# A hybrid encoder block on one core: the hidden layer of the feed-forward part formed in seven products from the third group on, with VectorE squaring its positive part in one pass

## The chip, the core and the metric

One core of a Trainium2 chip runs one program. The metric is the device time of an execution in microseconds (us). Engines: PE is TensorE (matmul), DVE VectorE, ACT ScalarE, POOL GpSimd, SP SyncE, which here only issues DMAs. They share no clock of work: each runs its own queue in order, and they meet through semaphores.

## What is computed

```python
h2 = modulate(rmsnorm(h_res, pre_ffn_g[l]), sh2, sc2)
f = jnp.square(jax.nn.relu(h2 @ w_ff1[l])) @ w_ff2[l]
h_res = h_res + gt2[:, None, :] * rmsnorm(f, post_ffn_g[l])
```

This is the channel sub-layer, the last third of a layer. The input h2 has 1024 tokens and 1024 features, w_ff1 is 1024 x 4096, w_ff2 4096 x 1024. Before it comes the mixing sub-layer (retention, stick-breaking attention, gates, an output projection), which the change leaves alone.

## The kernel before

Every fp32 product is made of three fp32r matmuls: each operand is kept as a high part (rounded by a copy) and a low part (the rest), and PE adds high x high, high x low and low x high into a PSUM bank. For weights ACT makes the high part (`w_high`, L1243) and POOL the low part (`low`, L489), 128 x 1024 elements, one **unit**, at a time; for the squares of the hidden layer ACT makes the high part (`f_high`, L1270) and DVE the low part (`f_low`, L1759).

The feed-forward part walks over 8 **groups** of 512 hidden features. A group has two halves.

- **Hidden** (`ff_hidden` on PE, L908, by way of `tile`, L543): 8 tiles, 4 blocks of 128 features by 2 halves of the tokens, each 8 chunks x 3 = 24 matmuls of 128 x 128 weights by 512 tokens, into the four banks `pg`. The operand is `r_hi`, `r_lo` (h2, transposed, 64 KB a partition). ACT takes each bank with Relu into `hid` and squares it there (`hidden`, L1253).
- **Second products** (`product`, L923): `hid` is cut in 2 x 2 blocks a11 to a22 and the 512 x 1024 part of w_ff2 likewise in b11 to b22, and seven products stand for eight (Strassen's scheme in Winograd's form). In PE's order they are P1, P4, P6, P5, P7, P3, P2, each 4 banks x 2 chunks x 3 = 24 matmuls. P1, P6, P7, P2 go to the banks `px`, P4, P5, P3 to `pg`; P6 and P7 add to what lies there, so each waits for the eviction of what came before. POOL makes the four sums of weight blocks, DVE the four sums of hidden blocks (a21, s2, a11, s2 again, L1781 to L1798) and the 32 evictions that add banks into `y` (`evict`, L1764). The last group makes its 16 tiles plainly (`ff_last`, L949).

Group 0 is written out, groups 1 to 6 are one loop on each engine, group 7 is `ff_last`. SP's queue (L404 to L427) loads the units of the next group as slots come free: two slots `raw` for w_ff1, four slots `w2` for w_ff2. The order on every queue is written out by hand. What makes ACT wait is gemm_done (PE's count of finished tiles) for a free slot, ff_sq for the squares, ff_s and ff_t for the sums.

One line says how a product waits; `free` gives the eviction that must be done:

```python
pe.wait_ge(ff_wlo, FF_UNITS * g + 4 + i + 1)
pe.wait_ge(ff_lo, FF_PRODS * g + i + 1)
```

After the last tile DVE and ACT normalise the rows of y and SP stores them (`finish`, `finish_last`).

## Time and profile before

| | |
|---|---|
| three executions | 1746.11, 1748.28, 1748.68 us, median 1748.28 |
| the profiled execution's own time | 1748.37 us |
| its span (first to last instruction) | 1746.6 us |
| busy in the span | PE 1709.1, DVE 905.0, ACT 561.3, POOL 604.2 us |
| mean granted clock of PE | 0.996 |
| feed-forward part | from about 1071 us to the end |

The profile is of one execution. Its page gives busy times, the chain of work that ended last (followed back from the last instruction), and groups of instructions by line with their mean duration and what ended the idle time before them. Beside it the trace can be asked for tables by stretches of time, for the instructions of one engine in order of time, and for those of one line. A matmul's duration of about 0.4 us there is its way through the pipeline; starts lie closer than that.

### The profile page before, as it was taken

Reading aid. Unit: us, or ns where it says so; the run is one execution under the profiler, and the core shown is the slowest. Engines: PE = TensorE matmul, PEld = TensorE weight load, DVE = VectorE, ACT = ScalarE, POOL = GpSimd, SP = SyncE. Lnnn points to the kernel's source line nnn. Section 1 sums busy time; section 2 is a strip of 40 time slices with the busy share of each in tenths; the row PEclk is TensorE's granted clock in tenths of the full one; section 3 lists DMA queues with packets and bytes.
Section 4 is the critical chain, followed back from the end, with each engine's and each line's share of the span. In section 5 each row is a group of like instructions: output and inputs, shape, how many; then the busy total and the mean of one; then the engine's idle time right before and its main releaser. Section 6 shows DMA issues by size and latency. Waiting matters only on the chain.

```text
span 1746.6 us, 25540 instructions
## 1 busy us (share of the span) xinstructions
PE 1709.1 (98%) x10016; PEld 1423.8 (82%) x10016; DVE 905.0 (52%) x1286; ACT 561.3 (32%) x952; POOL 604.2 (35%) x256
## 2 busy tenths in 40 slices
PE   5999999999999999999999999999999999999998
PEld 5877877777989898988888998788888888888876
DVE  6756666786446555652113277726261726252526
ACT  5556666110121212120002166333333333323242
POOL 2011111353323323233333742653535354444420
PEclk9999999999999999999999999999999999999999
DMA  8001001254401011113111545111111202020113
GB/s 346 21 25 50 25 26 61 93 209 169 149 25 52 25 52 37 41 37 133 48 48 48 175 164 192 48 49 55 42 60 36 72 24 72 24 85 13 71 66 127
DMA packets 38303, 135.16 MB, mean 77 GB/s; under 512 B 5956, under 2 KB 6852, under 8 KB 37704
## 3 DMA queue, kind: packets, MB, share of 16 engines
q1 hardware_dynamic: 30384, 109.66, 17.8%
q10 hardware_dynamic: 7832, 24.28, 3.7%
q8 instruction: 62, 1.02, 0.2%
q14 instruction: 25, 0.20, 0.0%
HBM read 121.33 MB, written 12.60 MB: 77 GB/s over the span
## 4 chain that ended last, share of the span: by engine, by line
PE 91%; DVE 3%; ACT 1%; POOL 1%; DMA 1%; issue 1%; SPq 0%; POOLq 0%; DVEq 0%; ACTq 0%
PE ps L551 17%; PE ps L549 17%; PE ps L550 16%; PE ps L932 5%; PE ps L934 5%; PE ps L933 5%; PE ps L635 3%; PE ps L636 3%; PE ps L637 3%; PE ps L811 2%; PE ps L688 2%; PE ps L813 2%; PE ps L812 2%; PE ps L652 1%; PE ps L670 1%
## 5 line engine op out<-in xcount | busy, mean ns | idle before, releaser
L451 POOL TENSOR_TENSOR w_hi<-raw,zero 128x1024 fp32r<-128x1024 f32 x58 | 113.4, 1955 | 463.8 <-PE ps L551 268.8
L551 PE MATMUL ps<-r_hi,w_lo 128*128 128x512 f32 x640 | 254.4, 397 | 0.0
L549 PE MATMUL ps<-r_hi,w_hi 128*128 128x512 f32 x640 | 252.3, 394 | 0.0
L550 PE MATMUL ps<-r_lo,w_hi 128*128 128x512 f32 x640 | 252.0, 394 | 0.0
L549 PE MATMUL ps<-w_hi,a_hi 128*128 128x256 f32 x768 | 219.3, 286 | 0.9 <-DVE a_lo L1659 0.6
L551 PE MATMUL ps<-w_hi,a_lo 128*128 128x256 f32 x768 | 215.7, 281 | 0.0
L550 PE MATMUL ps<-w_lo,a_hi 128*128 128x256 f32 x768 | 215.4, 281 | 0.0
L487 POOL TENSOR_TENSOR w_lo<-w,w_hi 128x1024 fp32r<-128x1024 f32 x39 | 100.2, 2570 | 213.7 <-ACT w_hi L1247 213.7
L1775 DVE TENSOR_TENSOR m<-m,ps 128x512 f32<-128x512 f32 x208 | 136.6, 684 | 72.0 <-PE ps L934 71.5
L932 PE MATMUL ps<-w_hi,f_hi 128*128 128x512 f32 x392 | 155.5, 397 | 0.4 <-issue 0.4
L934 PE MATMUL ps<-w_hi,f_lo 128*128 128x512 f32 x392 | 155.4, 396 | 0.0
L933 PE MATMUL ps<-w_lo,f_hi 128*128 128x512 f32 x392 | 155.3, 396 | 0.0
L453 POOL TENSOR_TENSOR w_lo<-raw,w_hi 128x1024 fp32r<-128x1024 f32 x58 | 145.9, 2516 | 4.5
L549 PEld LDWEIGHTS ps<-w_hi,a_hi 128*128 128x128 f32 x768 | 144.9, 189 | 2.6 <-issue 0.9
L550 PEld LDWEIGHTS ps<-w_lo,a_hi 128*128 128x128 f32 x768 | 144.9, 189 | 0.2
L550 PEld LDWEIGHTS ps<-r_lo,w_hi 128*128 128x128 f32 x640 | 120.1, 188 | 30.5
L551 PEld LDWEIGHTS ps<-w_hi,a_lo 128*128 128x128 f32 x768 | 144.7, 188 | 0.0
L549 PEld LDWEIGHTS ps<-r_hi,w_hi 128*128 128x128 f32 x640 | 120.1, 188 | 28.9 <-DVE r_lo L1706 0.5
L551 PEld LDWEIGHTS ps<-r_hi,w_lo 128*128 128x128 f32 x640 | 120.1, 188 | 28.4
L1475 DVE TENSOR_TENSOR_SCAN uu<-uu 128x512 f32<-128x512 f32 (+7 forms) x96 | 96.1, 1042 | 77.2 <-ACT uu L1077 76.9
L1762 DVE TENSOR_TENSOR f_lo<-hid,f_hi 128x1024 fp32r<-128x1024 f32 x35 | 51.5, 1472 | 149.7 <-ACT f_hi L1274 149.7
L464 POOL TENSOR_TENSOR w_lo<-raw,w_hi 128x1024 fp32r<-128x1024 f32 x16 | 42.5, 2664 | 232.4 <-ACT w_hi L999 204.9
(244 smaller groups left out, 3432.9 us busy)
## 6 DMA issues: line engine op xcount, KB each, us to landing
raw<-wstream SPq DMA_DIRECT2D x112, 512.0 KB, 3.6
ada_r<-ada_rows SPq DMA_DIRECT2D x32, 512.0 KB, 4.9
w<-wstream SPq DMA_DIRECT2D x32, 512.0 KB, 3.6
ada_s<-ada SPq DMA_DIRECT2D x7, 1024.0 KB, 17.1
m_dram<-m1s ACTq DMA_DIRECT2D x1, 4096.0 KB, 15.6
m<-m_dram ACTq DMA_DIRECT2D x1, 4096.0 KB, 13.0
x_dram<-m ACTq DMA_DIRECT2D x8, 512.0 KB, 4.9
rl_f<-x_dram ACTq DMA_DIRECT2D x2, 2048.0 KB, 9.7
```

Source lines behind the costliest of these rows:

```text
L451: nc.gpsimd.tensor_tensor(w_hi[:, slot, part], raw[:, h, :], zero[:, 0:1].broadcast_to([P, RAW]), ALU.add).then_inc(w_split, 1)
L453: nc.gpsimd.tensor_tensor(w_lo[:, slot, part], raw[:, h, :], w_hi[:, slot, part].bitcast(f32), ALU.subtract).then_inc(w_split, 1)
L487: return nc.gpsimd.tensor_tensor(out_, in0, in1, op)
L549: nc.tensor.matmul(outp, lh, rh, start=(k == 0), stop=False)
L550: nc.tensor.matmul(outp, lh, rl, start=False, stop=False)
L551: last = nc.tensor.matmul(outp, ll, rh, start=False, stop=(k == chunks - 1))
L635: nc.tensor.matmul(outp, hi, r_hi_, start=start, stop=False)
L932: nc.tensor.matmul(banks[:, t, :], fh, wh, start=(start and c == 0), stop=False, skip_group_check=not start)
L933: nc.tensor.matmul(banks[:, t, :], fh, wl, start=False, stop=False, skip_group_check=not start)
L934: last = nc.tensor.matmul(banks[:, t, :], fl, wh, start=False, stop=(c == 1), skip_group_check=not start)
L1475: V.tensor_tensor_scan(run, run, run, 1.0, ALU.mult, ALU.bypass).then_inc(scan_done, 1)
L1775: V.tensor_tensor(dst, dst, bank, op).then_inc(ff_ev, 1)
```

## The change

Groups 0 and 1 stay as they are, both written out. From group 2 on the hidden half too is done in seven products over 2 x 2 blocks: the input is cut by features (two halves of 512) and tokens, w_ff1's part by the same features and by 256 hidden features. In PE's order they are Q1, Q2, Q6, Q7, Q5, Q4, Q3 (Q7 goes into Q6's banks, which lie over Q1's; Q3 into Q5's), each 2 banks x 4 chunks x 3 = 24 matmuls.

- The seven input operands (three blocks of h2, four sums) are made once, in group 1: DVE forms the sums and their low parts in 4 rounds of 12 passes of 512 columns (`operand_sums`), the first five steps of round 0 already between the last evictions of group 0; ACT makes 16 high parts (`sums_high`); SP writes them to DRAM (`ops`, seven operands of 2 MB) in 6 DMAs of 1 MB and 16 of 0.5 MB. They use the second and third slot of f_hi and f_lo, so each round waits for the writes of the round before, and ACT's high parts of a22 and s2 in group 1 wait for the last ones.
- Each group reads all seven back through a ring of three slots of 2 MB (`ring`), which lies with four slots for w_ff1's units (the first two are `raw`) on the memory of r_hi and r_lo. The ring's first loads wait for the end of group 1's hidden half.
- w_ff1's blocks are v11 to v22, with sums u1, u2 and new values for v12 and v21 in place. POOL forms these four sums a group as well, and 7 low parts instead of 4 for it; b11's sum now goes to a buffer of its own (u1).
- ACT copies six banks to `hid`, the two of Q1 after Q1, again after Q6 and again after Q7. DVE adds the other banks in (`h_sum`) and then squares the positive part with one scalar_tensor_tensor, max(x, 0) * x. ACT's Relu and Square are gone from groups 2 to 7.
- The last group's tiles begin with the second half of the tokens, and x2 is read back by SP instead of ACT.

The diff, cut to its core:

```diff
+FF_PLAIN = 2
+Q1, Q2, Q6, Q7, Q5, Q4, Q3 = range(7)
+O_R11, O_R12, O_S2, O_S3, O_S1, O_R22, O_S4 = range(7)
+Q_WSLOT = (0, 1, 2, 3, 0, 1, 2)
+Q_RING = (0, 1, 2, 0, 1, 2, 0)
+P_WSLOT_W = (3, 0, 1, 2, 3, 0, 2)
+F_FREE_W = (8, 0, 4, 12, 16, 20, 24)
+W_UNITS, W_TILES, W_COPIES, W_ADDS, FF2_TILES = 14, 14, 6, 8, 28
+TL_W = TL_FF + FF_PLAIN * FF_TILES
...
+    ring = sb("ring", [P, 3, 2, 4, HALF], f32r, c)
+    w1s = sb("w1s", [P, 4, RAW], f32, c)
...
+    sp.wait_ge(n2_split, 32)
+    for o, k, th in ((O_R11, 0, 0), (O_R12, 4, 0), (O_R22, 4, 1)):
+        for part, a in enumerate((r_hi, r_lo)):
+            sp.dma_start(ops[o, :, part, :, :], a[:, k:k + 4, th * HALF:(th + 1) * HALF].bitcast(f32)).then_inc(r_out, 16)
...
+    for b in range(2):
+        w1_load(2, b, ff_wlo, FF_UNITS + 3 + b)
+    for k in range(4):
+        for pair, lo_done, to in ((0, 10, ops[O_S2:O_S3 + 1]), (1, 12, ops[O_S1:O_S4 + 1:2])):
+            sp.wait_ge(s_val, 12 * k + lo_done)
+            for part, f in enumerate((f_hi, f_lo)):
+                sp.dma_start(to[:, :, part, k, :].rearrange("s p n -> p s n"), f[:, 1 + pair, :, :].bitcast(f32)).then_inc(s_out[pair], 16)
+    sp.wait_ge(r_out, 16 * 6)
...
+        wu = w_unit(g)
+        sp.wait_ge(w1_t, 4 * (g - FF_PLAIN) + 1)
+        w1_load(g + 1, 0, ff_wlo, wu + Q1 + 1)
+        ring_load(3, *h_done(g, 0))
+        ring_load(4, *h_done(g, 1))
+        ring_load(5, *h_done(g, 2))
+        w1_load(g + 1, 1, ff_wlo, wu + Q7 + 1)
+        ring_load(6, *h_done(g, 3))
+        ring_load(1, *h_done(g, 4))
+        w1_load(g + 1, 2, ff_wlo, wu + Q4 + 1)
+        ring_load(2, *h_done(g, 5))
+        ring_load(0, *h_done(g, 6))
+        w1_load(g + 1, 3, ff_wlo, wu + Q3 + 1)
         for b, p in ((0, P5), (1, P7), (3, P3), (2, P2)):
-            ff_second(g, b, (ff_wlo, last + 4 + p + 1))
-        for c in range(2, 4):
-            load(unit(g, c), c - 2, (ff_wlo, FF_UNITS * g + c - 1))
+            ff_second(g + 1, b, (ff_wlo, wu + 7 + p + 1))
+    for o in range(3, 7):
+        ring_load(o, *h_done(FF_G - 1, o - 3))
...
+    def hidden_ahead(g, done):
+        n = 4 * (g - FF_PLAIN)
+        pool.wait_ge(ff_wlo, done)
+        if not isinstance(g, int) or g > FF_PLAIN:
+            pool.wait_ge(w1_t, n)
+        for b in range(2):
+            pool.wait_ge(w1_in[b], 16 * (g - 1))
+        add(u1, v12, v11, ALU.subtract).then_inc(w1_t, 1)
+        pool.wait_ge(w1_in[3], 16 * (g - 1))
+        pool.wait_ge(w1_t, n + 1)
+        add(u2, v22, u1, ALU.subtract).then_inc(w1_t, 1)
...
+    def hidden_units(g, sums):
+        n = 4 * (g - FF_PLAIN)
+        w_low(g, Q6, Q_WSLOT[Q6], u2)
+        add(v12, v22, v12, ALU.subtract).then_inc(w1_t, 1)
+        w_low(g, Q7, Q_WSLOT[Q7], v12)
+        w_low(g, Q5, Q_WSLOT[Q5], u1)
+        pool.wait_ge(ff_wlo, w_unit(g) + Q2 + 1)
+        pool.wait_ge(w1_t, n + 2)
+        add(v21, u2, v21, ALU.subtract).then_inc(w1_t, 1)
+        if sums:
+            for b in range(2):
+                pool.wait_ge(w2_in[b], 16 * g + 16)
+            pool.wait_ge(ff_wlo, w_unit(g) + Q5 + 1)
+            add(u1, b12, b11, ALU.subtract).then_inc(ff_t, 1)
+        w_low(g, Q4, Q_WSLOT[Q4], v21)
+        if sums:
+            pool.wait_ge(w2_in[3], 16 * g + 16)
+            pool.wait_ge(ff_t, 4 * g + 1)
+            add(t2, b22, u1, ALU.subtract).then_inc(ff_t, 1)
+        w_low(g, Q3, Q_WSLOT[Q3], v22)
+        if sums:
+            pool.wait_ge(ff_lo, FF_PRODS * g)
...
+    def w_group(g):
+        wu = w_unit(g)
+        hidden_units(g, True)
+        w_low(g, 7 + P1, P_WSLOT_W[P1], b11)
+        add(b12, b22, b12, ALU.subtract).then_inc(ff_t, 1)
+        w_low(g, 7 + P4, P_WSLOT_W[P4], t4)
+        w_low(g, 7 + P6, P_WSLOT_W[P6], t2)
+        w_low(g, 7 + P5, P_WSLOT_W[P5], u1)
+        w_low(g, 7 + P7, P_WSLOT_W[P7], b12)
+        w_low(g, 7 + P3, P_WSLOT_W[P3], b22)
+        w_low(g, 7 + P2, P_WSLOT_W[P2], b21)
+        hidden_ahead(g + 1, wu + W_UNITS)
...
+    def hidden_product(g, q, banks, start, free):
+        turn, slot = g - FF_PLAIN, Q_RING[q]
+        pe.wait_ge(ff_wlo, w_unit(g) + q + 1)
+        pe.wait_ge(ring_in[slot], (48 if slot == 0 else 32) * turn + 16 * (q // 3 + 1))
+        for m in range(2):
+            pe.wait_ge(*free(m))
+            for k in range(4):
+                wh, wl = (w[:, Q_WSLOT[q], k * 256 + m * P:k * 256 + (m + 1) * P] for w in (w_hi4, w_lo4))
+                xh, xl = (ring[:, slot, part, k, :] for part in range(2))
+                nc.tensor.matmul(banks[:, m, :], wh, xh, start=(start and k == 0), stop=False, skip_group_check=not start)
+                nc.tensor.matmul(banks[:, m, :], wl, xh, start=False, stop=False, skip_group_check=not start)
+                last = nc.tensor.matmul(banks[:, m, :], wh, xl, start=False, stop=(k == 3), skip_group_check=not start)
+            last.then_inc(h_mm, 1)
...
+    def hidden_products(g):
+        turn, ev = g - FF_PLAIN, FF_EVS * (g - 1)
+        x_banks, z_banks, y_banks, w_banks = px[:, 0:2, :], px[:, 2:4, :], pg[:, 0:2, :], pg[:, 2:4, :]
+        hidden_product(g, Q1, x_banks, True, lambda m: (ff_ev, ev + E_P2 + m + 1))
+        hidden_product(g, Q2, z_banks, True, lambda m: (ff_ev, ev + E_P2 + m + 3))
+        hidden_product(g, Q6, x_banks, False, lambda m: (h_copy, W_COPIES * turn + m + 1))
+        hidden_product(g, Q7, x_banks, False, lambda m: (h_copy, W_COPIES * turn + m + 3))
+        hidden_product(g, Q5, y_banks, True, lambda m: (ff_ev, ev + E_P3 + m + 1))
+        hidden_product(g, Q4, w_banks, True, lambda m: (ff_ev, ev + E_P3 + m + 3))
+        hidden_product(g, Q3, y_banks, False, lambda m: (h_add, W_ADDS * turn + m + 3))
+    def free_px(g):
+        turn = g - FF_PLAIN
+        return lambda t: (h_copy, W_COPIES * turn + t + 5) if t < 2 else (h_add, W_ADDS * turn + t - 1)
...
+    def sums_high(k):
+        for n, ready in ((0, 5), (1, 6), (2, 6), (3, 8)):
+            act.wait_ge(s_val, 12 * k + ready)
+            nc.scalar.activation(f_hi[:, 1 + n // 2, n % 2, :], sum_slot(n), ACT.Copy).then_inc(s_hi, 1)
...
+    def copied(g, n, c, th, bank):
+        turn = g - FF_PLAIN
+        act.wait_ge(h_mm, W_TILES * turn + (1, 2, 5, 6, 7, 8)[n])
+        nc.scalar.activation(hid[:, c, th * HALF:(th + 1) * HALF], bank, ACT.Copy).then_inc(h_copy, 1)
...
+    def hidden_part(g, seconds):
+        turn, tl, t1 = g - FF_PLAIN, w_tiles(g), 4 * (g - FF_PLAIN)
+        def h(q):
+            return h_mm, W_TILES * turn + 2 * q + 2
+        act.wait_ge(ff_lo, FF_PRODS * g)
+        unit_high(Q_WSLOT[Q6], u2, (gemm_done, tl + 8), (w1_t, t1 + 2))
+        copied(g, 0, 0, 0, px[:, 0, :])
+        unit_high(Q_WSLOT[Q7], v12, (gemm_done, tl), (w1_t, t1 + 3))
+        copied(g, 1, 1, 0, px[:, 1, :])
+        unit_high(Q_WSLOT[Q5], u1, h(Q1), (w1_t, t1 + 1))
+        f_high_w(g, P1, a11, ff_sq, 8 * g + 2)
+        unit_high(Q_WSLOT[Q4], v21, h(Q2), (w1_t, t1 + 4))
+        copied(g, 2, 2, 0, px[:, 0, :])
+        copied(g, 3, 3, 0, px[:, 1, :])
+        unit_high(Q_WSLOT[Q3], v22, h(Q6), (w1_in[3], 16 * (g - 1)))
+        copied(g, 4, 0, 1, px[:, 0, :])
+        copied(g, 5, 1, 1, px[:, 1, :])
+        unit_high(*seconds[0])
+        unit_high(*seconds[1])
+        f_high_w(g, P4, a22, ff_sq, 8 * g + 4)
+        if isinstance(g, int):
+            act.wait_ge(ff_sq, 8 * g + 6)
+            act.wait_ge(gemm_done, tl + 4)
+            nc.scalar.activation(f_hi[:, 2, :, :], a21, ACT.Copy).then_inc(ff_hi, 1)
...
+            return P_WSLOT_W[i], src, free, ready
+        hidden_part(g, (second(P1, b11, (h_mm, turn + 2 * Q7 + 2), w2_in[0], 16 * g + 16),
+                        second(P4, t4, (h_mm, turn + 2 * Q5 + 2), ff_t, 4 * g + 3),
+                        second(P6, t2, (h_mm, turn + 2 * Q4 + 2), ff_t, 4 * g + 2)))
+        f_high_w(g, P6, s2, ff_s, 4 * g + 2)
+        unit_high(*second(P5, u1, (h_mm, turn + 2 * Q3 + 2), ff_t, 4 * g + 1))
+        f_high_w(g, P5, a11, ff_s, 4 * g + 3)
+        unit_high(*second(P7, b12, (gemm_done, tl + 12), ff_t, 4 * g + 4))
+        f_high_w(g, P7, a21, ff_s, 4 * g + 1)
+        unit_high(*second(P3, b22, (gemm_done, tl + 16), w2_in[3], 16 * g + 16))
+        f_high_w(g, P3, s2, ff_s, 4 * g + 4)
+        unit_high(*second(P2, b21, (gemm_done, tl + 24), w2_in[2], 16 * g + 16))
+        f_high_w(g, P2, a12, ff_sq, 8 * g + 8)
...
+        def step(n, out_, in0, in1, op, after):
+            if after:
+                dve.wait_ge(s_val, 12 * k + after)
+            V.tensor_tensor(out_, in0, in1, op).then_inc(s_val, 1)
...
+        def low(m):
+            n = (0, 1, 2, 3)[m]
+            dve.wait_ge(s_hi, 4 * k + m + 1)
+            step(9 + m, s_(f_lo, n), sum_slot(n), s_(f_hi, n).bitcast(f32), ALU.subtract, 8 if m == 0 else 0)
+        for n in range(lo, hi):
+            if n == 0:
+                dve.wait_ge(*((s_out[0], 32 * k) if k else (gemm_done, TL_FF + 28)))
+                step(1, tmp, h11, l11, ALU.add, 0)
+            elif n == 1:
+                step(2, x3, tmp, h21, ALU.subtract, 1)
+            elif n == 2:
+                step(3, x3, x3, l21, ALU.subtract, 2)
+            elif n == 3:
+                step(4, x2_, h22, x3, ALU.subtract, 3)
+            elif n == 4:
+                step(5, x2_, x2_, l22, ALU.add, 4)
+            elif n == 5:
+                dve.wait_ge(*((s_out[1], 32 * k) if k else (gemm_done, TL_FF + 32)))
+                step(6, x1, x2_, tmp, ALU.add, 5)
+            elif n == 6:
+                step(7, x4, h12, x2_, ALU.subtract, 0)
+            elif n == 7:
+                step(8, x4, x4, l12, ALU.add, 7)
+            else:
+                low(n - 8)
     def ff_group(g):
         tl, ev = TL_FF + FF_TILES * g, FF_EVS * g
-        first = isinstance(g, int)
+        first = g == 0
...
+    def h_sum(g, n, dst, src, bank, op, copy):
+        turn = g - FF_PLAIN
+        dve.wait_ge(h_mm, W_TILES * turn + (3, 4, 9, 10, 11, 12, 13, 14)[n])
+        dve.wait_ge(h_copy, W_COPIES * turn + copy)
+        V.tensor_tensor(dst, src, bank, op).then_inc(h_add, 1)
+        dve.wait_ge(h_add, W_ADDS * turn + n + 1)
+        V.scalar_tensor_tensor(dst, dst, 0.0, dst, ALU.max, ALU.mult).then_inc(ff_sq, 1)
...
+    def hidden_sums(g):
+        for m in range(2):
+            h_sum(g, m, half(m, 0), half(m, 0), px[:, 2 + m, :], ALU.add, 1 + m)
+        f_low_w(g, 0, 0, a11)
+        for m in range(2):
+            h_sum(g, 2 + m, half(2 + m, 1), half(m, 1), pg[:, m, :], ALU.add, 5 + m)
+        h_sum(g, 4, half(0, 1), half(0, 1), pg[:, 2, :], ALU.subtract, 5)
+        f_low_w(g, 1, 1, a22)
+        h_sum(g, 5, half(1, 1), half(1, 1), pg[:, 3, :], ALU.subtract, 6)
...
+        hidden_sums(g)
+        dve.wait_ge(ff_sq, 8 * g + 6)
+        V.tensor_tensor(a21, a11, a21, ALU.subtract).then_inc(ff_s, 1)
+        h_sum(g, 6, half(2, 0), half(2, 0), pg[:, 0, :], ALU.add, 3)
+        dve.wait_ge(ff_wlo, w_unit(g) + 7 + P4 + 1)
+        dve.wait_ge(ff_s, 4 * g + 1)
+        V.tensor_tensor(s2, a22, a21, ALU.subtract).then_inc(ff_s, 1)
+        h_sum(g, 7, half(3, 0), half(3, 0), pg[:, 1, :], ALU.add, 4)
+        f_low_w(g, P6, P_FSLOT[P6], s2)
+        V.tensor_tensor(a11, s2, a11, ALU.add).then_inc(ff_s, 1)
+        for t in range(4):
+            evict(P1, t, px[:, t, :], 0, 0, ALU.add, ev)
+        dve.wait_ge(ff_sq, 8 * g + 8)
+        V.tensor_tensor(s2, a12, s2, ALU.subtract).then_inc(ff_s, 1)
+        f_low_w(g, P5, P_FSLOT[P5], a11)
...
```

## Rows read from the trace of the kernel before

**Rows 1.** The page: busy times; the chain that ended last, by engine.

```profile
PE 1709.1 (98%) x10016; PEld 1423.8 (82%) x10016; DVE 905.0 (52%) x1286; ACT 561.3 (32%) x952; POOL 604.2 (35%) x256
...
PE 91%; DVE 3%; ACT 1%; POOL 1%; DMA 1%; issue 1%; SPq 0%; POOLq 0%; DVEq 0%; ACTq 0%
```

**Rows 2.** By stretches: length; PE, PEld, DVE, ACT, POOL; clock; DMA share; GB/s.

```profile
1144.00:1228.00 84.00, 84.00 (x361) 67.54 (x360) 36.84 (x43) 28.18 (x34) 37.82 (x15) 1.00 0.15 51
...
1564.00:1648.00 84.00, 84.00 (x361) 67.53 (x361) 36.68 (x44) 28.19 (x34) 37.84 (x15) 1.00 0.14 50
```

**Rows 3.** PE's timeline (start, length): first matmuls of groups 1 and 3.

```profile
1143.80 0.40 PE L549 MATMUL ps<-r_hi,w_hi 128*128 128x512 f32 x1
...
1312.09 0.40 PE L549 MATMUL ps<-r_hi,w_hi 128*128 128x512 f32 x1
```

**Rows 4.** The waits from group 1 on: total us, times, longest.

```profile
PE ps L974 <- POOL w_lo L487: 0.7, 1, 0.7
```

**Rows 5.** ACT's groups of instructions in groups 1 to 6: busy us, mean ns.

```profile
L1258 ACT ACTIVATE hid<-ps 128x512 f32<-128x512 f32 x48 | 28.8, 600 | 158.6 <-PE ps L551 158.6
L1247 ACT ACTIVATE w_hi<-raw 128x1024 fp32r<-128x1024 f32 x24 | 25.5, 1063 | 87.0 <-PE ps L934 82.0 <-DMA raw<-wstream 4.9
```

**Rows 6.** POOL's timeline in group 1.

```profile
1157.49 2.41 POOL L487 TENSOR_TENSOR w_lo<-w,w_hi 128x1024 fp32r<-128x1024 f32 x1 [7.60 <-ACT w_hi L1247]
...
1167.38 2.41 POOL L487 TENSOR_TENSOR w<-w 128x1024 f32<-128x1024 f32 x1
1169.79 3.33 POOL L487 TENSOR_TENSOR w_lo<-hs,w_hi 128x1024 fp32r<-128x1024 f32 x1
...
1191.09 2.39 POOL L487 TENSOR_TENSOR w_lo<-w,w_hi 128x1024 fp32r<-128x1024 f32 x1 [8.79 <-ACT w_hi L1247]
```

**Rows 7.** DVE's timeline in group 1.

```profile
1144.00 0.69 DVE L1775 TENSOR_TENSOR m<-m,ps 128x512 f32<-128x512 f32 x1 [0.72 <-PE ps L934]
1168.79 2.07 DVE L1762 TENSOR_TENSOR f_lo<-hid,f_hi 128x1024 fp32r<-128x1024 f32 x1 [24.11 <-ACT f_hi L1274]
1170.79 3.41 DVE L1781 TENSOR_TENSOR hid<-hid 128x1024 f32<-128x1024 f32 x1
1184.70 1.23 DVE L1786 TENSOR_TENSOR hs<-hid 128x1024 f32<-128x1024 f32 x1 [10.49 <-ACT hid L1260]
1185.84 1.22 DVE L1762 TENSOR_TENSOR f_lo<-hid,f_hi 128x1024 fp32r<-128x1024 f32 x1
...
1191.60 0.69 DVE L1775 TENSOR_TENSOR m<-m,ps 128x512 f32<-128x512 f32 x1 [0.61 <-PE ps L934]
```

**Rows 8.** Single lines of DVE: duration ns, lowest/median/highest.

```profile
L1685 DVE SCALAR_TENSOR_TENSOR m<-m,tiny,rh_f x8: 1284/1285/3441, 1011.0 to 1064.6; 128x1024 f32<-128x1024 f32 x8
...
L1743 DVE TENSOR_TENSOR rh_f<-m,gtg x2: 691/692/693, 1737.4 to 1740.3; 128x512 f32<-128x512 f32 x2
...
L1752 DVE SCALAR_TENSOR_TENSOR m<-rh_f,tiny,rl_f x2: 747/750/752, 1742.3 to 1742.9; 128x512 f32<-128x512 f32 x2
```

**Rows 9.** DMA issues (us to landing), L1182's landings, a stretch at the start.

```profile
m<-m_dram ACTq DMA_DIRECT2D x1, 4096.0 KB, 13.0
...
out<-m SPq DMA_DIRECT2D x7, 512.0 KB, 2.6
...
DMA to landing us min/median/max: 2.6/4.9/8.8
...
5.00:10.00 5.00, 0.00 (x0) 0.00 (x0) 4.76 (x8) 2.31 (x3) 2.71 (x2) 1.00 1.03 411
```

**Rows 10.** By stretches, at the start and at the end (clock: third from last).

```profile
28.00:30.00 2.00, 2.00 (x16) 2.00 (x15) 1.02 (x1) 0.00 (x0) 0.00 (x0) 0.77 1.02 406
...
34.00:36.00 2.00, 2.00 (x11) 2.00 (x11) 1.64 (x2) 1.06 (x1) 0.00 (x0) 0.53 1.03 408
1739.00:1740.00 1.00, 0.50 (x3) 0.06 (x1) 0.93 (x2) 0.00 (x0) 0.00 (x0) 1.00 0.00 0
...
1742.00:1743.00 1.00, 0.00 (x0) 0.00 (x0) 0.96 (x4) 0.00 (x0) 0.00 (x0) 0.78 0.00 0
```

More of the change, by code:

```diff
@@ L1775, in evict @@
                     V.tensor_tensor(dst, dst, bank, op).then_inc(ff_ev, 1)
+                if not first:
+                    operand_sums(0, 5)
+                    for k in range(1, 3):
+                        operand_sums(k)
                 f_low(P1, a11)
```

372 lines of the change are left out of this document (248 added, 124 removed).

## The prediction

> **What bounds the kernel now.** I read the page's busy times and the chain of waits first [rows 1]: TensorE (PE) is busy in 98% of the span and holds 91% of the chain. The table by stretches then shows the feed-forward groups 1 and 6, of 84 us each: PE busy all of it, the clock whole, DVE 37 us, ACT 28, POOL 38 [rows 2]. PE's timeline gives the pace: group 1 begins at 1143.80 and group 3 at 1312.09, 720 matmuls in 168.29 us, 0.2337 us each [rows 3]. So matmuls removed there come off one for one, as long as operands are split and banks emptied in time. The only operand PE waits for is in the last group, 0.7 us [rows 4].
>
> **Matmuls.** Groups 2 to 7 form the hidden layer in 7 products of 24 matmuls (168) instead of 8 tiles of 24 (192): 6 x 24 x 0.2337 = **33.7 us off**. A product stays 5.6 us. Nothing is gained in groups 0 and 1.
>
> **Prices.** ACT: 1.06 us for 1024 columns, 0.60 for a bank [rows 5]. POOL: 2.41 for 1024 columns [rows 6]. DVE: bank plus SBUF, 512 columns, 0.69; SBUF only, 1024 columns, 1.23 (1.14 start to start) [rows 7]; of 512 columns 0.69, with a scalar and two tensors 0.75 [rows 8], so 0.65 a step when each waits for the last, an estimate. I count time from 1144.00, where DVE sees PE's last product of group 0 [rows 7]; PE itself runs 0.3 to 0.4 ahead, so it needs an operand that much before the round figure.
>
> **The two engines that exclude each other.** POOL is at work from 1167.38 to 1169.79; DVE's f_lo pass, begun at 1168.79, ends at 1170.86, one pass after POOL is done. POOL's next takes 3.33 instead of 2.41, and DVE's next, which came in behind it, 3.41 instead of 1.23 [rows 6, 7]. They alternate, a whole instruction each. The scalar_tensor_tensor form shows the same, 1.285 against 3.441 [rows 8]. An eviction from PSUM at 1191.60 beside POOL's 1191.09 keeps 0.69 [rows 6, 7]. So of the new work the sums (SBUF plus bank) are free of it, the squares (SBUF twice) and all operand sums are not. Both engines have idle time, but each wait falls in a queue.
>
> **A steady group (2 to 6), its start at 0.** POOL's list grows from 15 passes to 22 (14 low parts, 8 weight sums), 53 us of 78.4. DVE gains 8 sums and 8 squares; ACT loses 8 relu and 8 squares for 6 copies and 3 high parts. Walking the queues by the prices:
> - POOL: Q6 low 1.1 to 3.5 (its slot is free at 0), v12 to 6.0, Q7 low 7.1 to 9.5. The first square, due at 9.2, goes at 9.5; Q5 low 10.1 to 12.5; the second square 12.5 to 13.1; v21 to 15.4. ACT takes Q4's high part, which waits for v21, to 16.5, and only then the third copy, to 17.1. PE may not add Q7 to that bank before and wanted it at 16.4: **0.7 lost**.
> - POOL now runs without a pause from 16.5 to 41 (9 passes). The squares three to five, f_lo of a22 and square six each find one running and wait for it: their ends are 29.0, 32.0, 35.0, 38.5 and 41.6. Alone the sixth would end at 35.6. Behind it DVE's own queue (a21, sum, square, s2, sum, square, f_lo of s2) takes until 48.0.
> - POOL wants P5's low part at 47.7, DVE the new a11 at 47.9: POOL first, a11 ends at 51.4, the first eviction of P1 at 52.1. P6 adds into that bank and wanted it at 50.7: **1.4 lost**.
> - s2 for P3 waits for P7's low part (to 56.0), f_lo of a11 for P3's (57.1 to 59.5), the first eviction of P4 ends at 61.3, P5 wanted it at 57.7: **3.6 lost**.
> - The rest of the group meets no late operand: Q1's high part is let go 5.6 before the end, and 1.06 + 2.41 fit in, 1.6 to spare.
> Sum 5.7, so a group lasts 84.1, what it lasts now; 5 x 5.7 = **28.5 us on**. If DVE won the race at 47.9 (margin 0.2), P6 would wait for nothing and P5 for 2.3: 3.0 a group. Bounds 0 (no collision) and 7 (a further pass of 2.41 at one of them).
>
> **Last group.** Its 16 tiles are as before, fewer POOL passes: 0.7 at Q7 on; the wait of 0.7 [rows 4] remains. The load of x2 moves from ACT's queue to SP's, behind the last ring load, and lands well before its use some 25 us later: nothing.
>
> **Group 1, where the operands are made.** 48 DVE passes in four rounds k, 16 ACT copies, 16 writes of 0.5 MB; each round reuses the buffers, so it starts only when the round before has landed in DRAM. A write of 0.5 MB alone takes 2.6 us, in the stage before a median 4.9, at most 8.8 [rows 9]; for two together I take 2.6 + 1.3 = 3.9 (0.52 MB at 411 GB/s [rows 9]).
> - Round 0: six steps beside group 0's last evictions, two of them behind POOL's passes for units c2 and c3; first pair sent at 10.0, landed at 14.0.
> - Round 1 falls on P1's low part and the four weight sums, from 13.5 (1157.49 [rows 6]): five steps wait for five passes, step 5 ends at 28.5, the pair is sent at 31.8, landed at 35.8. ACT stands at its copies for this round until 31.
> - Round 2: one collision (P4's low part), lows done at 45.8. f_lo of P1 stands behind them, to 46.9; PE wanted it at 44.4: **2.6 lost**.
> - Round 3: starts at 50.1, pair landed at 60.6. ACT's high part of a22 waits for that, 61.7, f_lo 62.8, P4 starts at 62.9 instead of 52.6: **10.3 lost**. Later f_lo of a11 meets P3's low part once more: **1.3**.
> Sum **14.2 on**. Bounds: 6 (landing in 2.6 and round 1 ahead of POOL) and 21 (6 a landing, three in a chain). The six raw operand copies of 1 MB in group 0 and the first three ring loads (6.3 MB, 17 us from 62) end before their use; the weight units behind them on SP have over 10 us too.
>
> **Clock.** At the end PE is idle from 1739.5 and the granted clock is at half from 1742.6; in the start it ran at half (0.50) while busy, from about 29.1 to 35.9 [rows 10]. A standstill of 10 us should bring that on. Bounds: 0 and 6.8 us at half, 3.4 lost; no row lies nearer to either, I take the middle, **1.7**.
>
> **Ring loads.** Four of 2.1 MB must land in time, one per 5.6 us, each with 11.2 from issue: at 411 GB/s 5.1 plus some 2. The last, behind one weight unit, lands at 30.4 against 33.9: nothing. At 381 GB/s (4.19 MB in 13.0 less 2 [rows 9]) still nothing. The Trainium skill ("DMA: Bandwidth & Descriptors", Specifications) gives about 358 GB/s of HBM per core. By that figure the slack falls to some 1 us, with the sum unchanged, which makes the fourth rival likelier; the trace's 411 speaks against it.
>
> **Sum.** The profiled execution took 1748.37 (span 1746.6), 0.1 above the median shown. 1748.4 - 33.7 + 28.5 + 0.7 + 14.2 + 1.7 = **1759.8**.
>
> **Rivals.**
> 1. The likeliest, above: locks and the landing chain eat more than the gain. 0.38. Own range 1752 to 1769.
> 2. The same collisions, but DVE wins at 47.9 and a landing is quicker: 3.0 x 5 + 0.7 + 11 + 0.7 = 27.4, so **1742**, 1736 to 1750. The margin of 0.2 speaks for it; both queues at 1170.79 going to the one that was waiting speaks against. 0.31. The Trainium skill ("SBUF — State Buffer", Who interferes with whom) says that issue order decides who blocks. By it POOL, first in line, would keep the turn, the sum as above.
> 3. Operands are early nearly everywhere: 1 us a group and 6 to 10 in group 1: 1748.4 - 33.7 + 5 + 0.7 + 8 = **1728**, down to 1718. For it: DVE and POOL have idle time; against: the alternation [rows 6, 7]. 0.17.
> 4. Ring loads late: at 300 GB/s each takes 7.0, the last lands at 37 against 33.9, 3 to 4 us a group on top of 1: **1775**. Against: 411 GB/s over ten microseconds. 0.07.
> 5. The standstills of 3.6 us in each steady group halve the clock too; the idle stretch before it fell at the end, 1739.5 to 1742.6, is no longer [rows 10]. 5 x 3 on top of 1: **1775**. 0.07.
> That the products don't get fewer can't be: they are counted in the code.
>
> **Chances.** A difference counts from 0.2%, 3.5 us, about what a measurement of this kernel can tell. Faster: 0.21 of rival 2 and all of 3, 0.38. Within: 0.10 of rival 2 and 0.01 of 1, 0.11. Slower: 0.37 of 1, and 4 and 5, 0.51. Range 1727 to 1770: leaves out the lower part of 3 (0.1) and the upper of 4 and 5 (0.1).
>
> **What would show it.** In the table by stretches, groups 2 to 6 near 84 us with PE idle 5 to 6 of it; in the waits, PE at the second products' line waiting for DVE's evictions (P6, P5), and at the hidden products' for ACT's copy; in DVE's timeline squares of about 3 us instead of 0.75. In group 1, PE idle some 10 us before its P4, released by DVE's f_lo behind ACT and SP's writes. Groups of 79 us or less would prove me wrong on the locks, PE passing P4 of group 1 within 3 us wrong on the chain; idle before a hidden product released by DMA would be rival 4.

## The result, and the profile after

The changed kernel takes **1751.94 us** (median of 11 executions, 1748.86 to 1756.06), the kernel before 1748.16 in the same comparison (11 executions): ratio **1.0025** [1.0016, 1.0034]. It is slower, by 3.8 us; forecast were 11.4. The profiled execution took 1753.33 us, its span is 1751.5.

The page's busy times and its chain by engine, against [rows 1]:

```profile
PE 1686.4 (96%) x9872; PEld 1401.3 (80%) x9872; DVE 1081.1 (62%) x1430; ACT 548.7 (31%) x926; POOL 725.0 (41%) x298
...
PE 72%; DVE 9%; POOL 8%; issue 7%; ACT 2%; DMA 1%; DVEq 0%; SPq 0%; POOLq 0%; ACTq 0%
```

The 144 matmuls are gone and PE is 22.7 us less busy, but the span is 4.9 longer: PE now stands still. In the chain it went from 91% to 72%, and DVE, POOL and issue took its place. By stretches, groups 1, 2, 3 and 6, against [rows 2] (columns as there):

```profile
1142.91:1242.46 99.55, 88.63 (x362) 70.60 (x361) 81.26 (x90) 36.91 (x50) 43.38 (x17) 0.93 0.51 195
1242.46:1324.70 82.24, 79.06 (x337) 62.99 (x336) 59.51 (x59) 24.59 (x27) 58.33 (x23) 1.00 0.59 230
1324.70:1408.50 83.80, 80.60 (x337) 64.11 (x336) 60.35 (x59) 24.57 (x27) 58.29 (x23) 0.98 0.58 226
1575.81:1659.35 83.54, 80.36 (x337) 63.97 (x336) 60.28 (x59) 24.61 (x27) 58.27 (x23) 0.98 0.58 224
```

Group 1 takes 99.55 us where it took 84.15 (168.29 / 2, [rows 3]): **15.4 on**. Groups 2 to 6 take 82.24, 83.80, 83.56, 83.75 and 83.54, 416.9 together where they took 420.7: only **3.8 off**. The last group's PE work took 90.42 and takes 84.33: **6.1 off**. With the start 0.9 earlier and 0.4 more behind the last matmul that is the 4.9, to the rounding. The waits of PE from group 1 on say where it stands; DVE's line is the evictions:

```profile
PE ps L1091 <- DVE m L2200: 15.3, 5, 3.1
PE ps L1091 <- issue: 10.9, 2, 8.8
```

Five waits of 3.1 us are the one before P5 in each steady group. The two under "issue" are before P1 and P4 of group 1, 2.1 and 8.8. No wait on a DMA appears: the ring of operands is in time. The wait of [rows 4] is gone.

**A steady group.** DVE's and POOL's timelines in group 4, which PE starts at 1408.50; what the prediction counts from its zero is counted from 1408.70.

```profile
1435.09 2.10 DVE L2170 SCALAR_TENSOR_TENSOR hid<-hid 128x512 f32<-128x512 f32 x1
1437.17 0.69 DVE L2168 TENSOR_TENSOR hid<-hid,ps 128x512 f32<-128x512 f32 x1
1437.89 2.12 DVE L2170 SCALAR_TENSOR_TENSOR hid<-hid 128x512 f32<-128x512 f32 x1
...
1446.80 2.19 DVE L2170 SCALAR_TENSOR_TENSOR hid<-hid 128x512 f32<-128x512 f32 x1
...
1455.09 3.42 DVE L2211 TENSOR_TENSOR hid<-hs,hid 128x1024 f32<-128x1024 f32 x1
1458.43 2.47 DVE L2200 TENSOR_TENSOR m<-m,ps 128x512 f32<-128x512 f32 x4
1460.82 3.37 DVE L2215 TENSOR_TENSOR hs<-hid,hs 128x1024 f32<-128x1024 f32 x1
1464.11 3.39 DVE L2179 TENSOR_TENSOR f_lo<-hid,f_hi 128x1024 fp32r<-128x1024 f32 x1
1467.43 2.47 DVE L2200 TENSOR_TENSOR m<-m,ps 128x512 f32<-128x512 f32 x4
```

```profile
1436.60 2.86 POOL L582 TENSOR_TENSOR w_lo<-w,w_hi 128x1024 fp32r<-128x1024 f32 x1
1439.42 2.86 POOL L582 TENSOR_TENSOR w<-w 128x1024 f32<-128x1024 f32 x1
...
1454.91 2.51 POOL L582 TENSOR_TENSOR w_lo<-w1s,w_hi 128x1024 fp32r<-128x1024 f32 x1 [6.48 <-ACT w_hi L1551]
1460.71 5.72 POOL L582 TENSOR_TENSOR w_lo<-w,w_hi 128x1024 fp32r<-128x1024 f32 x2 [3.28 <-ACT w_hi L1551]
```

Four of the eight squares (the third to the sixth) meet a pass of POOL in full and take 2.10 to 2.19; the first two take 0.86 and 0.88, the last two, with POOL at rest, 0.69. A sum from a PSUM bank takes 0.69 as ever. POOL's P5 pass comes in at 1454.91, DVE's a11 at 1455.09, and DVE is held for 3.42 instead of 1.22. Both passes of the next pair (s2 for P3, f_lo of a11) find POOL at work and take 3.37 and 3.39; only then come the four evictions of P4, and PE starts P5 at 1468.16, where it was ready at 1464.94.

**Group 1.** DVE's timeline: the first steps of round 1 (five meetings with POOL), of rounds 2 and 3, and the two passes that let P1 and P4 go; then PE's first matmul of each.

```profile
1157.97 1.58 DVE L2056 TENSOR_TENSOR fs_f<-r_hi,r_lo 128x512 f32<-128x512 f32 x1 [3.06 <-DMA ops<-f_lo]
1159.59 2.81 DVE L2056 TENSOR_TENSOR fs_f<-fs_f,r_hi 128x512 f32<-128x512 f32 x1
...
1180.42 0.69 DVE L2056 TENSOR_TENSOR fs_f<-r_hi,r_lo 128x512 f32<-128x512 f32 x1 [4.85 <-DMA ops<-f_lo]
...
1188.66 1.22 DVE L2099 TENSOR_TENSOR f_lo<-hid,f_hi 128x1024 fp32r<-128x1024 f32 x1
1191.79 1.27 DVE L2056 TENSOR_TENSOR fs_f<-r_hi,r_lo 128x512 f32<-128x512 f32 x1 [1.91 <-DMA ops<-f_lo]
...
1204.83 1.22 DVE L2099 TENSOR_TENSOR f_lo<-hid,f_hi 128x1024 fp32r<-128x1024 f32 x1 [1.64 <-ACT f_hi L1495]
```

```profile
1189.98 0.47 PE L1091 MATMUL ps<-w_hi,f_hi 128*128 128x512 f32 x1 [2.11 <-issue]
...
1206.15 0.77 PE L1091 MATMUL ps<-w_hi,f_hi 128*128 128x512 f32 x1 [8.81 <-issue]
```

Each round waits for the writes of the round before it, and P4 starts 63.24 us after the group's first matmul (1206.15 - 1142.91).

**The clock.** By stretches, around the wait before P5 in group 3 (PE idle from 1381.2 to 1384.39), in group 4 (PE takes up work again at 1468.16) and in group 2 (at 1302.12), equal waits all three:

```profile
1382.00:1384.00 2.00, 0.00 (x0) 0.00 (x0) 2.00 (x2) 0.42 (x1) 0.66 (x1) 1.00 0.22 68
1384.00:1386.00 2.00, 1.61 (x7) 1.29 (x8) 2.00 (x4) 0.00 (x0) 0.00 (x0) 0.94 0.68 242
1386.00:1388.00 2.00, 2.00 (x6) 1.61 (x5) 2.00 (x4) 0.00 (x0) 0.00 (x0) 0.50 0.00 0
1388.00:1390.00 2.00, 2.00 (x8) 1.54 (x8) 2.00 (x4) 0.00 (x0) 0.00 (x0) 0.71 0.00 0
```

```profile
1466.00:1468.00 2.00, 0.00 (x0) 0.00 (x0) 2.00 (x2) 0.20 (x1) 0.42 (x1) 0.92 0.22 57
1468.00:1470.00 2.00, 1.84 (x4) 1.49 (x5) 2.00 (x5) 0.00 (x0) 0.00 (x0) 0.50 0.55 207
```

```profile
1302.00:1304.00 2.00, 1.89 (x8) 1.56 (x9) 2.00 (x5) 0.00 (x0) 0.00 (x0) 1.00 0.58 211
1304.00:1306.00 2.00, 2.00 (x11) 1.59 (x10) 2.00 (x3) 0.00 (x0) 0.00 (x0) 1.00 0.00 0
```

In groups 3 to 6 the granted clock falls to half, the 1.2 GHz level, for about 3.4 us. In groups 3 and 5 it falls 1.3 to 1.4 us after PE has taken up work again, in groups 4 and 6 some 0.5 us before that, while PE still stands. In group 2 it stays whole, and that group is 1.3 to 1.6 us shorter than the others.

### The profile page after: what moved, and what is told of

Its sections match the earlier page's. It is cut to its first block, busy times and chain, and to the rows that moved or that the text cites. A ratio compares the mean times of both kernels' runs of the same rounds, so it can differ in the third digit from the quotient of the medians.

```text
span 1751.5 us, 25587 instructions
## 1 busy us (share of the span) xinstructions
PE 1686.4 (96%) x9872; PEld 1401.3 (80%) x9872; DVE 1081.1 (62%) x1430; ACT 548.7 (31%) x926; POOL 725.0 (41%) x298
## 4 chain that ended last, share of the span: by engine, by line
PE 72%; DVE 9%; POOL 8%; issue 7%; ACT 2%; DMA 1%; DVEq 0%; SPq 0%; POOLq 0%; ACTq 0%
PE ps L714 12%; PE ps L716 11%; PE ps L715 11%; POOL w_lo L582 4%; PE ps L1091 3%; PE ps L1093 3%; PE ps L1092 3%; PE ps L800 3%; PE ps L801 3%; PE ps L802 3%; POOL w1s L582 2%; PE ps L976 2%; PE ps L853 2%; PE ps L978 2%; PE ps L977 2%
## 5 line engine op out<-in xcount | busy, mean ns | idle before, releaser
L1091 PE MATMUL ps<-w_hi,f_hi 128*128 128x512 f32 x440 | 179.6, 408 | 26.6 <-DVE m L2200 15.3
L1093 PE MATMUL ps<-w_hi,f_lo 128*128 128x512 f32 x440 | 178.2, 405 | 0.0
L1092 PE MATMUL ps<-w_lo,f_hi 128*128 128x512 f32 x440 | 177.8, 404 | 0.0
L1134 PE MATMUL ps<-ring,w_hi 128*128 128x512 f32 x336 | 133.4, 397 | 0.7
L1136 PE MATMUL ps<-ring,w_hi 128*128 128x512 f32 x336 | 132.9, 395 | 0.0
L1135 PE MATMUL ps<-ring,w_lo 128*128 128x512 f32 x336 | 132.6, 395 | 0.0
L1091 PEld LDWEIGHTS ps<-w_hi,f_hi 128*128 128x128 f32 x440 | 85.4, 194 | 51.0 <-DVE m L2200 17.5
L2200 DVE TENSOR_TENSOR m<-m,ps 128x512 f32<-128x512 f32 x160 | 99.8, 677 | 15.0 <-PE ps L1093 14.5
L582 POOL TENSOR_TENSOR w_lo<-w1s,w_hi 128x1024 fp32r<-128x1024 f32 x35 | 87.3, 2496 | 38.6 <-ACT w_hi L1551 38.6
L2168 DVE TENSOR_TENSOR hid<-hid,ps 128x512 f32<-128x512 f32 x48 | 32.8, 683 | 112.5 <-PE ps L1136 112.5
L1092 PEld LDWEIGHTS ps<-w_lo,f_hi 128*128 128x128 f32 x440 | 85.6, 195 | 20.4
## 6 DMA issues: line engine op xcount, KB each, us to landing
m<-m_dram ACTq DMA_DIRECT2D x1, 4096.0 KB, 12.7
```

The source lines that it names most:

```text
L582: return nc.gpsimd.tensor_tensor(out_, in0, in1, op)
L1091: nc.tensor.matmul(bank, fh, wh, start=start, stop=False, skip_group_check=skip)
L1092: nc.tensor.matmul(bank, fh, wl, start=False, stop=False, skip_group_check=skip)
L1093: return nc.tensor.matmul(bank, fl, wh, start=False, stop=stop, skip_group_check=skip)
L1134: nc.tensor.matmul(banks[:, m, :], wh, xh, start=(start and k == 0), stop=False, skip_group_check=not start)
L1135: nc.tensor.matmul(banks[:, m, :], wl, xh, start=False, stop=False, skip_group_check=not start)
```

## The experiments

All start from the changed kernel. The ratio is to the kernel before, which ran beside each on the same chip (medians 1747.5 to 1747.8).

| run | us | ratio | group 1 | a steady group |
|---|---|---|---|---|
| the change itself | 1751.94 | 1.0025 [1.0016, 1.0034] | 99.6 | 82.2 to 83.8 |
| evictions first | 1729.32 | 0.9900 [0.9883, 0.9916] | 98.9 | 79.0 |
| no squares | 1727.30 | 0.9883 [0.9866, 0.9899] | 98.6 | 78.6 |
| squares on ACT | 1728.89 | 0.9897 [0.9882, 0.9912] | 99.4 | 78.5 to 78.8 |
| GpSimd later | 1730.80 | 0.9904 [0.9888, 0.9919] | 99.8 | 78.9 |
| f_lo early | 1754.52 | 1.0038 [1.0023, 1.0052] | 99.4 | 83.6 to 85.0 |
| rounds split | 1738.78 | 0.9956 [0.9940, 0.9973] | 84.1, twice | 83.6 to 83.8 |
| small writes | 1749.18 | 1.0015 [1.0005, 1.0024] | 94.8 | 83.5 to 84.9 |
| sums later | 1752.97 | 1.0034 [1.0022, 1.0045] | 97.8 | 82.3 to 85.0 |
| no sums | 1747.32 | 0.9998 [0.9989, 1.0008] | 90.7 | 83.6 to 85.0 |
| both left out | 1739.11 | 0.9950 [0.9933, 0.9966] | 84.7 | 82.3 to 85.1 |
| three edits | 1719.72 | 0.9843 [0.9830, 0.9857] | 84.1, twice | 79.0 |

The last two columns are of one profiled execution each. Where PE waits before P5, the clock falls in some groups and not in others, and that alone moves the five steady groups together by up to 3 us (416.9 in the change, 418.4 to 419.8 in the five other runs with such a wait in all five). What an edit did to group 1 is therefore read from that column and not from the time.

**The steady groups: the order of DVE's queue.**

```diff
-    dve.wait_ge(ff_sq, 8 * g + 8)
-    V.tensor_tensor(s2, a12, s2, ALU.subtract).then_inc(ff_s, 1)
     f_low_w(g, P5, P_FSLOT[P5], a11)
     for t in range(4):
         evict(P4, t, pg[:, t, :], 1, 0, ALU.subtract, ev)
+    dve.wait_ge(ff_sq, 8 * g + 8)
+    V.tensor_tensor(s2, a12, s2, ALU.subtract).then_inc(ff_s, 1)
```

> Only the order of VectorE's queue in a steady group is changed: the low part of a11 and the four evictions of P4 come before the sum s2 for P3. Theory of the locks (VectorE's passes with two SBUF inputs wait for a whole GpSimd pass each, and the evictions of P4 stand behind two such passes): the wait of 3.2 us before P5 goes in all five groups, with it the fall of the clock after it (1.3 to 1.7 us in four of them), so each steady group lasts about 79.0 us instead of 83.4 and the kernel takes 17 to 19 us less than the one before, ratio 0.990. Rival (VectorE has too much work there, whatever the order): the wait turns up again before P7 or P3, groups stay at 83 us, ratio 1.002.

DVE's timeline of that run in its group 3, from the end of P1's evictions:

```profile
1370.90 3.38 DVE L2179 TENSOR_TENSOR f_lo<-hid,f_hi 128x1024 fp32r<-128x1024 f32 x1
1374.20 2.47 DVE L2200 TENSOR_TENSOR m<-m,ps 128x512 f32<-128x512 f32 x4
1376.59 1.21 DVE L2218 TENSOR_TENSOR hs<-hid,hs 128x1024 f32<-128x1024 f32 x1
```

f_lo of a11 still meets POOL (3.38), but one meeting fewer stands ahead of the evictions, which begin 5.7 after P1's instead of 9.0. The wait is gone, a group takes 78.96, and two moved lines turn the change from 0.25% slower to 1% faster: in the profiled executions the five groups give 416.9 - 5 x 79.0 = 22 us, and the medians lie 22.6 apart.

**The squares.** Two runs ask whether they make DVE late: they are left out in groups 2 to 7 (the sums enter the second products as they are, neither cut at zero nor squared), or ACT makes them as before the change, Relu and Square in place, which undoes the change's second part alone.

```diff
-    V.scalar_tensor_tensor(dst, dst, 0.0, dst, ALU.max, ALU.mult).then_inc(ff_sq, 1)
+    dve.sem_inc(ff_sq, 1)
```

> The squares of groups 2 to 7 are left out (the sums are passed on as they are), so VectorE has 8 passes of 512 columns less in a group, 6 us of the 84. Theory of the locks: each of these six squares before the end of the hidden half stood behind a GpSimd pass and set it back by 0.45; without them VectorE comes to a11 at about 44 instead of 50, the wait before P5 and the small one before Q7 go, groups last 78.7 us, ratio 0.988 to 0.990. Rival (the wait before P5 is GpSimd's or ScalarE's lateness, or VectorE's work after the hidden half): the wait stays at about 3 us, ratio 1.001 to 1.002.

```diff
-    V.scalar_tensor_tensor(dst, dst, 0.0, dst, ALU.max, ALU.mult).then_inc(ff_sq, 1)
...
+    act.wait_ge(h_add, W_ADDS * (g - FF_PLAIN) + n + 1)
+    nc.scalar.activation(part, part, ACT.Relu).then_inc(ev_act, 1)
+    act.wait_ge(ev_act, EA_FF + 8 * g + n + 1)
+    nc.scalar.activation(part, part, ACT.Square).then_inc(ff_sq, 1)
```

> The second part of the change undone alone: ACT makes the squares of the hidden blocks (Relu, then Square, both in place) and VectorE none; the seven hidden products stay. Theory of the exclusive turns: VectorE loses eight passes a group of which six stood for 2.1 us each behind GpSimd; the wait before P5 is 0 to 1 us, a steady group lasts 78.6 to 80, ratio 0.988 to 0.992. ACT is 8 x 1.3 us fuller and may let a high part go later. Rival (the wait before P5 is made at the end of the group only, the squares have no part in it): wait near 3, ratio 1.002.

Without squares PE waits for nothing in a steady group, which takes 78.55 to 78.60: the matmuls' own time. With them on ACT it is the same but for one group of 78.77. So the first part of the change, fewer products, is worth 1.0% as it stands, and the second, the squares on DVE, took it back. The one pass of DVE is not dear by itself (0.69 with POOL at rest, against two passes of ACT); it is dear in a queue in which it waits for POOL. (Both expectations that speak of six squares behind POOL count too many: it is four, as shown above.)

**Is it DVE's load, or the meetings?** Nothing is taken off DVE here and its order stays; ACT makes the high part of a21 first and only then, once DVE has done f_lo of a11, the two high parts of weights that POOL's next two passes wait for.

```diff
+    f_high_w(g, P7, a21, ff_s, 4 * g + 1)
+    act.wait_ge(ff_lo, FF_PRODS * g + 4)
     unit_high(*second(P7, b12, (gemm_done, tl + 12), ff_t, 4 * g + 4))
-    f_high_w(g, P7, a21, ff_s, 4 * g + 1)
```

> VectorE's order is that of the changed kernel; ACT holds the high parts of P7's and P3's weight units, and with them GpSimd's low parts, until VectorE has done f_lo of a11. Nothing is taken off VectorE. Theory of the exclusive turns: s2 and f_lo of a11 run beside no pass of GpSimd, 1.2 us each instead of 3.4, the first eviction of P4 ends near 55 instead of 59.45, the wait before P5 (3.1) is gone and the clock stays whole in the steady groups, ratio 0.989 to 0.991. Rival (VectorE's queue is simply too long there, GpSimd has no part): eviction near 59, wait near 3, ratio 1.002.

DVE's timeline and POOL's of that run, its group 4 (PE starts it at 1400.75):

```profile
1453.07 1.21 DVE L2216 TENSOR_TENSOR hs<-hid,hs 128x1024 f32<-128x1024 f32 x1
1454.21 1.21 DVE L2180 TENSOR_TENSOR f_lo<-hid,f_hi 128x1024 fp32r<-128x1024 f32 x1
1455.34 2.47 DVE L2201 TENSOR_TENSOR m<-m,ps 128x512 f32<-128x512 f32 x4
```

```profile
1447.16 2.51 POOL L582 TENSOR_TENSOR w_lo<-w1s,w_hi 128x1024 fp32r<-128x1024 f32 x1 [6.47 <-ACT w_hi L1551]
1456.72 5.75 POOL L582 TENSOR_TENSOR w_lo<-w,w_hi 128x1024 fp32r<-128x1024 f32 x2 [7.05 <-ACT w_hi L1551]
```

The same instructions in the same order take 1.21 instead of 3.37 and 3.39, for POOL starts its two passes 56.0 after the group's start instead of 52.2, behind them; the evictions begin 54.6 after the group's start, not 58.9, and the wait is gone. With DVE's list of work unchanged, two meetings fewer are enough. So DVE's load alone does not make the wait; the meetings in its queue do, and it goes when the last two go (here), when the evictions stand ahead of one of them (evictions first) or when the squares go with theirs.

**Group 1: what pins P4.** First, is the wait before P1 a loss of its own?

```diff
     operand_sums(0, 5)
-    for k in range(1, 3):
-        operand_sums(k)
+    operand_sums(1)
 f_low(P1, a11)
+if not first:
+    operand_sums(2)
```

> In group 1 VectorE forms the low part of a11 before round 2 of the operand sums instead of after it. Theory of the chain (the rounds with their landings set when P4 can begin, the wait before P1 is only its first instalment): the 2.3 us before P1 go, the wait before P4 grows from 9.0 to 11.3, P4 begins at the same time, and only the clock's fall after the first wait (about 1.6 us) is saved: 1 to 2 us less than the change, ratio 1.001 to 1.002. Rival (two separate waits): P4's wait stays at 9.0 and 4 us are saved, ratio 1.000.

The wait before P1 is gone and the one before P4 is 12.7 us: P4 starts 63.24 after the group's start, as in the changed kernel to the hundredth. Its start is set by the chain of rounds alone, and whatever PE gains ahead of it is given back there. The time was missed: not 1 to 2 us less than the change but 2.6 more. Group 1 is only 0.2 shorter; in the profiled execution the steady groups are 2.8 longer together, since the clock fell in all five, in group 2 for 6.8 us.

The chain has two ingredients, landings of writes and meetings with POOL. Writes of 8 partitions instead of 128:

```diff
...
-    sp.dma_start(to[:, :, part, k, :].rearrange("s p n -> p s n"), f[:, 1 + pair, :, :].bitcast(f32))
+    sp.dma_start(to[:, 0:8, part, k, :].rearrange("s p n -> p s n"), f[0:8, 1 + pair, :, :].bitcast(f32))
...
```

> Leaves out: of the sixteen writes of operand sums in group 1 only 8 of 128 partitions are written (the rest of the region is filled in group 0 with 8 MB copied from h2's operands, which ends before group 1). The rounds wait for these small writes exactly as before for the 0.5 MB ones. Landing-chain theory: sent-to-landed falls from 4.2, 6.0, 4.2 and 4.2 us to about 2 each, four in a chain, so P4 of group 1 starts at 53 to 56 instead of 63.2 after the group's start, and the group lasts 87 to 91 instead of 99.5; ratio 0.995 to 0.998. Rival (the chain is made of collisions and ACT's and VectorE's own passes, landings are a small part): P4 at 60 or later, group 1 of 95 or more.

P4 starts at 59.17, between what both sides expected. The idle times on writes in front of the three rounds and of ACT's a22 fell from 3.06, 4.85, 1.91 and 3.84 to 1.35, 1.28, 0.16 and 2.08, by 8.8 in all, but rounds that start earlier meet more passes of POOL: 4.7 more time in meetings. 8.8 - 4.7 is the 4.1 measured. Group 1 is 4.8 shorter than in the change, the median only 2.8, since the steady groups are 2.6 longer together.

POOL's four sums moved behind round 1:

```diff
     pool.wait_ge(ff_wlo, first_low)
+    if isinstance(g, int) and g == 1:
+        pool.wait_ge(s_val, 24)
```

> GpSimd makes group 1's four sums of weight blocks only after VectorE has done round 1 of the operands, so they fall on the landing of round 1 instead of on its steps. Theory of the exclusive turns: round 1 loses four collisions of 2.1 us, its second pair is sent near 23 instead of 31.3; round 2 meets one or two of the moved sums; f_lo of P1 is early (no wait before P1), P4 starts at 56 to 60 instead of 63.2, group 1 lasts 92 to 96; ratio 0.997 to 1.000. Rival (the chain of landings alone sets P4's start): P4 at 62 or later, group 1 near 99.

A miss for both sides: 61.56, and the kernel is no faster than the change. DVE's timeline of that run: the first two steps of round 1, then all that meets POOL in round 2.

```profile
1157.78 1.57 DVE L2058 TENSOR_TENSOR fs_f<-r_hi,r_lo 128x512 f32<-128x512 f32 x1 [3.07 <-DMA ops<-f_lo]
1159.39 0.69 DVE L2058 TENSOR_TENSOR fs_f<-fs_f,r_hi 128x512 f32<-128x512 f32 x1
...
1170.27 2.69 DVE L2058 TENSOR_TENSOR fs_f<-r_hi,r_lo 128x512 f32<-128x512 f32 x1 [3.29 <-DMA ops<-f_lo]
1173.00 2.78 DVE L2058 TENSOR_TENSOR fs_f<-fs_f,r_hi 128x512 f32<-128x512 f32 x1
1175.81 2.78 DVE L2058 TENSOR_TENSOR fs_f<-fs_f,r_lo 128x512 f32<-128x512 f32 x1
1178.62 2.77 DVE L2058 TENSOR_TENSOR fs_f<-r_hi,fs_f 128x512 f32<-128x512 f32 x1
```

Four meetings left round 1 and four came in round 2: the block of passes moved, and DVE ran into it one landing later. What was gained, 1.7 us, is nearly all the landing after round 1 (3.29 of idle time instead of 4.85). So the sums were left out altogether (group 1's second products then run on unsummed blocks of weights), and once more together with the small writes:

```diff
+    if isinstance(g, int) and g == 1:
...
+        pool.sem_inc(ff_t, 4)
+        return
     add(b11, b12, b11, ALU.subtract).then_inc(ff_t, 1)
```

> Leaves out GpSimd's four sums of weight blocks in group 1 (its products there run on unsummed blocks); nothing else is changed. This is the run in which the four meetings of round 1 are gone and can't come back in round 2. Theory that meetings are half of the chain: round 1's lows end near 24 instead of 32.7 after the group's start, round 2 meets at most one low part, f_lo of P1 is early, P4 starts at 53.5 to 56 instead of 63.2, group 1 lasts 86 to 90 instead of 99.5; ratio 0.993 to 0.997. Rival (something else pins P4, such as the writes' order in SP's queue): P4 at 60 or later.

> Leaves out the same four sums, and writes only 8 of 128 partitions of the operand sums in group 1 (the rest is filled in group 0). If meetings and landings are all of the chain: P4's operands are there by 52, TensorE waits nowhere in group 1, which lasts 84.2 to 85; ratio 0.991 to 0.994 (the waits before P5 in the steady groups stay). Rival: a wait before P4 of over 3 us stays.

PE's timeline of the first, the start of P4 (group 1 starts at 1144.27):

```profile
1199.08 0.76 PE L1097 MATMUL ps<-w_hi,f_hi 128*128 128x512 f32 x1 [4.25 <-issue]
```

P4 starts at 54.81, and the 8.4 gained are 6.7 of meetings and 1.8 of the landing after round 1. With both left out the wait is 0.3 and the group takes 84.7: take meetings and most of the landings away, and nothing of the chain is left that PE would feel. Group 1 itself was 90.7 in the first, a little above its expectation, since the clock still halved around the wait of 4.25. Both ratios were missed on the slow side (0.9998 for 0.993 to 0.997, 0.9950 for 0.991 to 0.994): group 1 gave back 8.8 and 14.8, the medians only 4.6 and 12.8, for in the profiled executions the steady groups are 2.9 and 1.7 longer together.

**Giving the chain two groups.** Rounds 0 and 1 in group 1, rounds 2 and 3 in group 2, hidden products from group 3 on. That costs the 24 matmuls saved in one group (5.6 us).

```diff
-FF_PLAIN = 2
+FF_PLAIN = 3
...
-    for k in range(1, 3):
-        operand_sums(k)
+    operand_sums(2 * g - 2, 5)
+    operand_sums(2 * g - 1)
...
```

> The four rounds of operand sums are spread over two plain groups (rounds 0 and 1 in group 1, rounds 2 and 3 in group 2), and the seven products begin with group 3. Theory of the chain: two rounds fit under a hidden half, so groups 1 and 2 last 84.2 us each with at most 1 us of waiting, group 1 gives back 15.4 us; one group less gains 5.6 less and one less pays 4.8. Sum against the change -15.4 + 5.6 - 4.8 + 0.5 = -14, ratio about 0.994. Rival (the rounds cost VectorE and ScalarE the same wherever they stand): the waits are split between the two groups, 10 us or more together, ratio 1.000 or above.

Groups 1 and 2 take 84.1 each with no wait, and the kernel gains 13.2 on the change. Here the unsaved matmuls cost little, for the steady group that group 2 was had lasted 82.2; once the steady groups last 79.0 they cost about 5. Then all together, with ACT's copy for Q7 ahead of Q4's high part, which waits for POOL:

```diff
-    unit_high(Q_WSLOT[Q4], v21, h(Q2), (w1_t, t1 + 4))
     copied(g, 2, 2, 0, px[:, 0, :])
+    unit_high(Q_WSLOT[Q4], v21, h(Q2), (w1_t, t1 + 4))
```

> Three edits together: VectorE's f_lo of a11 and its evictions of P4 ahead of the s2 for P3; rounds 0 and 1 of the operands in group 1 and rounds 2 and 3 in group 2 (hidden products from group 3 on); ACT's third copy ahead of Q4's high part. Theory of the exclusive turns and the landing chain: every wait of TensorE that the change brought is gone (P5's 3.1, Q7's 0.3, group 1's 2.1 and 8.8), groups 1 and 2 last 84.1 each and groups 3 to 6 78.6 each, the clock stays whole, span 1715 to 1720, ratio to the kernel before 0.982 to 0.985. Rival (the waits only move on to the next product or to the ring loads, and what the second edit gained is partly what the first gained): groups 3 to 6 of 80 or more, ratio 0.988 or above.

Its page, and by stretches group 1 and the first two steady groups:

```profile
PE 1680.7 (98%) x9896; PEld 1399.2 (81%) x9896; DVE 1057.5 (62%) x1414; ACT 552.9 (32%) x933; POOL 708.0 (41%) x291
```

```profile
1142.17:1226.32 84.15, 84.15 (x361) 67.68 (x360) 66.23 (x68) 32.45 (x42) 38.49 (x15) 1.00 0.29 100
...
1310.47:1389.43 78.96, 78.85 (x338) 63.01 (x337) 57.05 (x59) 24.74 (x27) 58.84 (x23) 1.00 0.62 240
1389.43:1468.40 78.97, 78.90 (x337) 63.01 (x336) 56.99 (x59) 24.75 (x27) 58.80 (x23) 1.00 0.61 239
```

**1719.72 us**, 1.6% faster than the kernel before, with no wait of PE left from group 1 on. The steady groups are 0.4 longer than the 78.55 of the run without squares: the wait before Q7 is gone, but now P6 starts 0.27 late, too short for the list of waits. So the third edit gave a steady group nothing (79.0 with it and without it): what PE no longer waits before Q7 it waits before P6, whose start is pinned to DVE's queue as P4's in group 1 was to the rounds.

## Why the prediction was wrong in size and right in sign

The sign and the mechanism were right, and so were the places but one: PE idle at P5 behind DVE's evictions, at P4 of group 1 behind the chain, nothing at the ring; the wait at P6 did not come. The size was not: 11.4 forecast, 3.8 measured (4.9 in the profiled span).

- **Matmuls, 33.7 off: right.** A steady group without waits takes 78.55 in two runs, 5.60 under 84.15.
- **The waits of a steady group, 5.7 each and 28.5 in all: the step that failed.** Its terms 0.7, 1.4 and 3.6 add up to how late P5 starts, and it is set by one event, DVE's first eviction of P4: walked to end at 61.3, with PE there at 55.6 if nothing had held it (57.7 - 0.7 - 1.4). It ended at 59.4 (1467.43, its first 0.67, less 1408.70), so **the walk had it 1.9 too late**. The group with a whole clock lost 3.7 (82.25 - 78.55) where the walk had 5.7: 5 x 2.0 = 10 us too much.
- **Where the walk of DVE's queue went wrong.** Squares three, four, five and six end at 28.5, 31.3, 34.1 and 40.3 instead of 29.0, 32.0, 35.0 and 41.6. From one square to the next the walk steps 3.0; measured are 2.8, the distance at which POOL's passes start when the two take turns (1436.60, 1439.42). DVE's a11 came to its race at 46.4, walked at 47.9, and the first eviction of P1 ended at 50.4 (1458.43, its first 0.67, less 1408.70), walked to 52.1. Small errors of one sign add up over a row of turns.
- **P6, 1.4: did not come;** PE wanted that bank at 50.6, 0.2 after its eviction. This is a sign of the same error and not a sum of its own: by the walk's times P5 could not start before 61.3, so without a wait at P6 it would have waited 5.0 instead of 3.6. The run with three edits shows such a trade, the 0.3 at Q7 for 0.3 at P6.
- **P5, 3.6: 3.2,** with luck in the size: the eviction came 1.9 earlier than walked, but PE, held less at Q7 (0.3 instead of 0.7) and not at P6, came 1.5 earlier too (56.2 instead of 57.7). The place and the cause were right, and the race for a11 went to POOL (1454.91 against 1455.09, the forecast margin of 0.2), against rival 2. (The Trainium skill, "SBUF — State Buffer", Who interferes with whom, has issue order decide who blocks; by it POOL, 0.18 earlier, goes first, and the trace agrees.)
- **The clock in the steady groups, 0: wrong.** Rival 5's mechanism came, with 0.07: it adds 1.3 to 1.6 us in four of five groups, 5.6 in all, where the rival had 3 a group. By luck it hid half of the error in the waits. The five groups: -10 + 5.6 is, to the rounding, the -4.3 by which they beat the forecast (84.24 against 83.38 on average).
- **Group 1, 14.2 + 1.7: right in the sum,** 15.4. f_lo of P1 ended at 46.8 (forecast 46.9), f_lo of a22 at 62.9 (62.8), P4 started at 63.0 (62.9). The chain behind it is partly luck: the first pair of round 1 was walked to land at 35.8 and landed at 37.3, and round 2, walked with one meeting (P4's low part), had none, since POOL's pass at 1178.05 was over when the round began at 1180.42. Late by 1.5 and short by about as much, the two cancel. The waits are 2.3 and 9.0 instead of 2.6 and 10.3, because P1 itself ran 1.6 us longer at the low clock; ahead of a start that is pinned, that costs nothing. Behind P4's start the clock took 2.6, and the later wait of 1.3 did not come.
- **Last group, 0.7 on: too much by 1.2.** The wait of [rows 4] did not come, which the prediction had kept, and Q7's was 0.3. Why the first went no run asks.

Put together for the profiled spans: the five steady groups lose 28.0 of matmuls (420.7 - 5 x 78.55) and get 24.1 back in waits and clock, group 1 adds 15.4, the last group takes 6.1 off, start and end 0.5: 4.9 on. Of the 6.5 between that and the forecast, 4.3 lie in the steady groups, 1.2 in the last, 0.5 in group 1 and 0.5 at the start and the end. What ate the gain is thus 24.1 in five groups whose P5 is pinned to DVE's queue and 15.4 in the one group that makes the operands.

Rival 4 had no part. While the first ring loads and the weights behind them ran, DMA moved 433 GB/s:

```profile
1212.60:1222.80 10.20, 10.20 (x46) 8.18 (x45) 10.20 (x12) 4.02 (x4) 4.82 (x3) 1.00 1.01 433
```

The Trainium skill's 358 GB/s a core ("DMA: Bandwidth & Descriptors", Specifications) is below what this stretch shows over ten microseconds; the measurement decides.

## What to carry to other kernels

Where two engines take turns at SBUF, an added pass costs what it waits for, not what it takes: here 0.69 became 2.1, and squares that were to spare ACT two passes turned 1.0% faster into 0.25% slower. In the queue of the engine that frees the bottleneck's banks, what frees them stands first and what feeds a later product behind it; that order was worth 22 us. And look for the start that is pinned, in a chain of rounds or in a steady group: ahead of it nothing is gained, and waits ahead of it must not be added up as if each were a price of its own. In the chain a meeting that was moved turned up in the next round, and giving the chain a second group, with one group of matmuls left unsaved, paid 13 us net, more than any single link that was shortened.

## What was not expected

- After equal waits of 3.06 us PE's clock fell to half in some steady groups and not in others. Groups with that wait last 82.2 to 82.3, 83.5 to 83.8 or 84.9 to 85.1 us over all the runs; the stretch at half clock is absent in the first kind (group 2 above), 3.4 us long in the second (groups 3 and 4 above) and 6.8 in the third. What decides between them stays open.
- The first pair of writes of round 1 had landed 6.0 us after it was sent, those of the other three rounds 4.2; the prediction had 3.9. DVE's idle time behind them was 4.85, and 3.06 to 3.29 in the two runs that sent them 8 us earlier. The cause wasn't tried.
- A write of 8 partitions instead of 128 still left 1.3 us of idle time in front of a round that was otherwise ready: that part of a landing is not made of bytes.
